# RWKV groups: the next group's key projection right behind the states, other scratch buffers at a group's end, and both squares on ScalarE

## The reference, cut to what matters

```python
def rwkv7_mixer(p, h, v_first, vres, n_ctx, mu, ...):
    shifted = concat([nbr_mean_seq(p[:, :n_ctx]), nbr_mean_grid(p[:, n_ctx:])])
    p = p + mu * (shifted - p)                       # "mixing" with neighbours
    r, k, v, wd_f, wd_b, ad_f, ad_b, gd = split_sizes(p, RWKV_SIZES)
    if vres is not None:
        v = v + (v_first - v) * sigmoid(v0 + (h @ v_down) @ v_up)
    g = sigmoid(gd) @ g_up
    kk = heads(k * k_k, H)
    kk = kk * rsqrt(sum(kk * kk, -1) + L2_EPS)       # square number one
    ...                                              # decays and a, per direction
    o = bidir_prefix(rwkv7_scan, dirs[0], dirs[1], s0, n_ctx)
    var = mean(square(o - mean(o)), -1)              # square number two
    o = merge_heads((o - mean) * rsqrt(var + eps)) * lnx_w + lnx_b
    bonus = (sums over r * k_d * r_k) * v_h
    y = (o + bonus) * g
```

## Time and profile before

| | |
|---|---|
| three runs | 2348.57, 2356.98, 2362.03 us |
| the profiled execution's own time | 2357.53 us |
| its span | 2355.7 us |
| mean granted TensorE clock | 0.962 of full |
| PE (TensorE matmul) busy | 2165.9 us (92%) |
| PEld (weight load) | 1829.6 us (78%) |
| DVE (VectorE) | 1349.7 us (57%) |
| ACT (ScalarE) | 970.6 us (41%) |
| POOL (GpSimd) | 371.9 us (16%) |

### The profile page before, as it was taken

One profiled execution on the slowest core, in us unless ns is written; L12 is line 12 of the kernel. 1 busy time (PEld: TensorE's weight loads), 2 busy tenths in 40 slices (PEclk: granted clock), 3 DMA queues, 4 the chain that ended last, 5 costly groups with the idle time before them and its releaser, 6 DMA issues. The chain is left out here.

```text
span 2355.7 us, 50157 instructions
## 1 busy us (share of the span) xinstructions
PE 2165.9 (92%) x21268; PEld 1829.6 (78%) x21268; DVE 1349.7 (57%) x1956; ACT 970.6 (41%) x1385; POOL 371.9 (16%) x347
## 2 busy tenths in 40 slices
PE   7887999999999999999999998878898988998998
PEld 3565778778787688878888877667887877898998
DVE  5436575665566443464444466477666555567666
ACT  4534233232554232342322347444443454445444
POOL 0002322422333200000000000131232255100000
PEclk9898999999999999999999998999999999999999
DMA  7531413423211223322222233200000122355553
GB/s 282 201 125 59 154 65 110 142 69 135 81 58 55 77 94 98 139 81 98 99 95 94 98 137 106 84 21 29 20 12 29 33 77 68 116 184 189 178 179 126
DMA packets 64734, 241.32 MB, mean 102 GB/s; under 512 B 7296, under 2 KB 8448, under 8 KB 63104
## 3 DMA queue, kind: packets, MB, share of 16 engines
q1 hardware_dynamic: 62064, 218.66, 27.3%
q10 hardware_dynamic: 2448, 19.46, 2.2%
HBM read 231.80 MB, written 6.29 MB: 101 GB/s over the span
## 5 line engine op out<-in xcount | busy, mean ns | idle before, releaser
L397 PE MATMUL psum<-normed_high,weights_high 128*128 128x512 f32 (+1 forms) x1552 | 568.7, 366 | 16.7 <-DVE weight_ring_parts L1042 13.7
L1042 DVE TENSOR_TENSOR weight_ring_parts<-weight_ring,weights_high 128x1024 fp32r<-128x1024 f32 (+1 forms) x327 | 413.2, 1264 | 261.3 <-ACT weights_high L1559 254.1
L398 PE MATMUL psum<-normed_low_part,weights_high 128*128 128x512 f32 (+1 forms) x1552 | 554.4, 357 | 0.0
L399 PE MATMUL psum<-normed_high,weight_ring_parts 128*128 128x512 f32 (+1 forms) x1552 | 553.1, 356 | 0.0
L1559 ACT ACTIVATE weights_high<-weight_ring 128x1024 fp32r<-128x1024 f32 (+1 forms) x327 | 339.9, 1040 | 187.6 <-PE psum L399 136.7
L397 PEld LDWEIGHTS psum<-normed_high,weights_high 128*128 128x128 f32 x1552 | 305.3, 197 | 74.2 <-DVE weight_ring_parts L1042 25.4
L398 PEld LDWEIGHTS psum<-normed_low_part,weights_high 128*128 128x128 f32 x1552 | 305.4, 197 | 40.4 <-issue 2.3
L399 PEld LDWEIGHTS psum<-normed_high,weight_ring_parts 128*128 128x128 f32 x1552 | 303.9, 196 | 40.5
L470 PEld LDWEIGHTS psum<-work 64*64 64x64 f32 x7040 | 233.9, 135 | 35.3 <-issue 24.5
L470 PE MATMUL psum<-work 64*64 64x64 f32 (+1 forms) x7040 | 243.0, 224 | 19.6 <-issue 7.6
L397 PE MATMUL psum<-hidden_high,weights_high 128*128 128x512 f32 (+1 forms) x512 | 172.4, 337 | 3.7 <-DVE hidden_low L1501 3.7
(11 more groups left out here) (241 smaller groups left out, 3217.4 us busy)
## 6 DMA issues: line engine op xcount, KB each, us to landing
weight_ring<-in_weights SPq DMA_DIRECT2D x407, 512.0 KB, 3.5
x_scratch<-work ACTq DMA_DIRECT2D x2, 2048.0 KB, 10.0
weight_ring<-in_weights SPq DMA_DIRECT2D x16, 256.0 KB, 2.6
work<-x_scratch ACTq DMA_DIRECT2D x2, 2048.0 KB, 9.3
work<-in_ret_constants ACTq DMA_DIRECT2D x2, 1152.0 KB, 14.9
work<-in_x ACTq DMA_DIRECT2D x1, 2048.0 KB, 10.0
work<-in_small_weights ACTq DMA_DIRECT2D x1, 1152.0 KB, 5.1
constants<-in_constants ACTq DMA_DIRECT2D x1, 1024.0 KB, 7.2
```

The costliest lines, as they stand in the source:

```text
L397: mm(ps, w[0][:, cols], x[0], start=first, stop=False)
L398: mm(ps, w[0][:, cols], x[1], start=False, stop=False)
L399: return mm(ps, w[1][:, cols], x[0], start=False, stop=last)
L1042: tt(ring_r[:, i % RING, o], ring[:, i % RING, o], high[:, n % HIGHS, o].bitcast(F32), ALU.subtract).then_inc(vec_split.sem, vec_split.ste ...
```

## The change

The key projection of group c+1 moves ahead of the low-rank matmuls on TensorE, and its copies, its mix and its `kk` move ahead of the low-rank work on ScalarE and VectorE. The products of line 1263 stay where they were. The group's end of groups 0 to 2 works in buffers of the two directions that are free by then (`T_OUT`, `T_SQ`, `T_RMS`, `T_BONUS`), and so do two scratch tiles of the values in layer 1, so the pads of `RW_SCR` stay zero and are written once per layer. ScalarE makes both squares in place of GpSimd, and waits for `kk` in its order ahead of a table load and the decays. Group 0 of a layer also has `keys(0)` ahead of `low_rank_parts(0)` on VectorE.

```diff
 # TensorE
 for c in range(NT):
-    project(big, big_filled, split("rw", l, c, 1), ("rkv", l, c, 1))
     if c == 0:
+        project(big, big_filled, split("rw", l, c, 1), ("rkv", l, c, 1))
         eng.wait_ge(act_rwkv.sem, act_rwkv.at("small ready", l))
         for d in range(2):
             low_rank(c, d)
     project(big, big_filled, split("rw", l, c, 0), ("rkv", l, c, 0), lo)
-    eng.wait_ge(pool_rwkv.sem, pool_rwkv.at("kk squared", l, c))
+    eng.wait_ge(act_rwkv.sem, act_rwkv.at("kk squared", l, c))
     big.start_at(2)
     sum_over(bones, wk(RW_SQ), ("kk norm", l, c))
     project(second, big_filled, split("rw", l, c, 2), ("rkv", l, c, 2))
...
-    big.start_at(0)
+    big.start_at(0 if c == NT - 1 else 3)
     if c < NT - 1:
+        project(big, big_filled, split("rw", l, c + 1, 1), ("rkv", l, c + 1, 1))
         low_rank(c + 1, 0)
...
-    eng.wait_ge(pool_rwkv.sem, pool_rwkv.at("centred squared", l, c))
-    sum_over(bones, wk(RW_SCR + 512)[:, lo:N], ("var", l, c), w)
+    eng.wait_ge(act_rwkv.sem, act_rwkv.at("centred squared", l, c))
+    sum_over(bones, wk(T_SQ[c])[:, lo:N], ("var", l, c), w)

 # VectorE
+def keys(c):
+    k = wk(RW_RKV + 512)
+    mix(4 + c, k, ("mixed", l, 4 + c))
+    ts(wk(RW_KK), k, pcol(l, "kk", c), None, ALU.mult)...
+keys(0)
 low_rank_parts(0)
 decayed(0)
 for c in range(NT):
-    mix(4 + c, k, ("mixed", l, 4 + c))
-    ts(wk(RW_KK), k, pcol(l, "kk", c), None, ALU.mult)...
...
     vec_rwkv.also(("centred", l, c))
     if c < NT - 1:
+        keys(c + 1)
         low_rank_parts(c + 1)

 # ScalarE
+def keys_squared(c):
+    eng.wait_ge(vec_rwkv.sem, vec_rwkv.at("kk raw", l, c))
+    act(wk(RW_SQ), wk(RW_KK), ACT.Square)...
-if c > 0:
-    eng.wait_ge(pool_rwkv.sem, pool_rwkv.at("pads rwkv", l, c - 1))
-project(1)
 if c == 0:
+    project(0, 1)
     low_rank(c, 0)
     low_rank(c, 1)
+    keys_squared(0)
     tables(LOG_EXP)
     decays(c)
-project(0)
+project(c, 0)
...
 weights_high(split_at["rw", l, c, 2] + 4)
+eng.wait_ge(vec_rwkv.sem, vec_rwkv.at("centred", l, c))
+act(wk(T_SQ[c])[:, lo:N], wk(T_OUT[c])[:, lo:N], ACT.Square)...
 if c < NT - 1:
     tables(SIGMOID)
+    project(c + 1, 1)
     low_rank(c + 1, 0)
     low_rank(c + 1, 1)
+    keys_squared(c + 1)
     tables(LOG_EXP)

 # GpSimd
 for c in range(NT):
     neighbours(4 + c)
-    eng.wait_ge(vec_rwkv.sem, vec_rwkv.at("kk raw", l, c))
-    tt(wk(RW_SQ), wk(RW_KK), wk(RW_KK), ALU.mult)...
     neighbours(c)
...
-    eng.wait_ge(vec_rwkv.sem, vec_rwkv.at("centred", l, c))
-    tt(wk(RW_SCR + 512)[:, lo:N], wk(RW_SCR)[:, lo:N], wk(RW_SCR)[:, lo:N], ALU.mult)...
-    if c < NT - 1:
-        eng.wait_ge(vec_rwkv.sem, vec_rwkv.at("drained", "gate", l, c))
-        pads(c)
```

More of the change, by code:

```diff
@@ L92 @@
     0, 1024, 1536, 2048, 2560, 3072, 3584, 4096, 4608, 5120, 6144, 6656, 7168)
+T_OUT, T_SQ, T_RMS, T_BONUS = (
+    [a] * 3 + [RW_SCR + 512 * i] for i, a in enumerate((RW_D[0] + RR, RW_D[0] + TT, RW_D[1] + RR, RW_D[1] + TT)))
+T_VGATE, T_VDIFF = RW_D[1] + TT, RW_D[1] + RR
 HG_F, HG_Q, HG_K, HG_A, HG_V, HG_T = 6144, 10240, 14336, 18432, 24576, 26624
@@ L1293, in values_gated @@
                         eng.wait_ge(act_rwkv.sem, act_rwkv.at("vgate sigmoid", l, c))
-                        tt(wk(RW_SCR + 512), wk(RW_SCR + 512), wk(RW_SCR), ALU.mult).then_inc(vec_rwkv.sem, vec_rwkv.step())
+                        tt(wk(T_VDIFF), wk(T_VDIFF), wk(T_VGATE), ALU.mult).then_inc(vec_rwkv.sem, vec_rwkv.step())
                         eng.wait_ge(vec_rwkv.sem, vec_rwkv.n)
-                        tt(vv, vv, wk(RW_SCR + 512), ALU.add).then_inc(vec_rwkv.sem, vec_rwkv.step(("v ready", l, c)))
+                        tt(vv, vv, wk(T_VDIFF), ALU.add).then_inc(vec_rwkv.sem, vec_rwkv.step(("v ready", l, c)))
                         eng.wait_ge(vec_rwkv.sem, vec_rwkv.n)
@@ L1376, in _ @@
                     eng.wait_ge(out_filled.sem, out_filled.at("O", l, c, 0))
-                    cp(wk(RW_SCR)[:, lo:N], outb.get("O", l, c, 0)[:, lo:N]).then_inc(vec_rwkv.sem, vec_rwkv.step(("drained", "O", l, c, 0)))
+                    cp(wk(T_OUT[c])[:, lo:N], outb.get("O", l, c, 0)[:, lo:N]).then_inc(vec_rwkv.sem, vec_rwkv.step(("drained", "O", l, c, 0)))
                     eng.wait_ge(vec_rwkv.sem, vec_rwkv.n)
                     eng.wait_ge(out_filled.sem, out_filled.at("O", l, c, 1))
-                    tt(wk(RW_SCR)[:, lo:N], wk(RW_SCR)[:, lo:N], outb.get("O", l, c, 1)[:, lo:N], ALU.add).then_inc(vec_rwkv.sem, vec_rwkv.step(("drained", "O", l, c, 1)))
+                    tt(wk(T_OUT[c])[:, lo:N], wk(T_OUT[c])[:, lo:N], outb.get("O", l, c, 1)[:, lo:N], ALU.add).then_inc(vec_rwkv.sem, vec_rwkv.step(("drained", "O", l, c, 1)))
                     eng.wait_ge(vec_rwkv.sem, vec_rwkv.n)
@@ L1383, in _ @@
                     if c < NT - 1:
+                        keys(c + 1)
                         low_rank_parts(c + 1)
                     eng.wait_ge(big_filled.sem, big_filled.at("bonus", l, c))
-                    tt(wk(RW_SCR + 1536)[:, lo:N], big.get("bonus", l, c)[:, 0:w], vv[:, lo:N], ALU.mult).then_inc(vec_rwkv.sem, vec_rwkv.step(("drained", "bonus", l, c)))
+                    tt(wk(T_BONUS[c])[:, lo:N], big.get("bonus", l, c)[:, 0:w], vv[:, lo:N], ALU.mult).then_inc(vec_rwkv.sem, vec_rwkv.step(("drained", "bonus", l, c)))
                     eng.wait_ge(vec_rwkv.sem, vec_rwkv.n)
                     eng.wait_ge(act_rwkv.sem, act_rwkv.at("rwkv rms", l, c))
-                    tt(wk(RW_SCR)[:, lo:N], wk(RW_SCR)[:, lo:N], wk(RW_SCR + 1024)[:, lo:N], ALU.mult).then_inc(vec_rwkv.sem, vec_rwkv.step())
+                    tt(wk(T_OUT[c])[:, lo:N], wk(T_OUT[c])[:, lo:N], wk(T_RMS[c])[:, lo:N], ALU.mult).then_inc(vec_rwkv.sem, vec_rwkv.step())
                     eng.wait_ge(vec_rwkv.sem, vec_rwkv.n)
-                    ts(wk(RW_SCR)[:, lo:N], wk(RW_SCR)[:, lo:N], pcol(l, "lnw", c), pcol(l, "lnb", c), ALU.mult, ALU.add).then_inc(vec_rwkv.sem, vec_rwkv.step())
+                    ts(wk(T_OUT[c])[:, lo:N], wk(T_OUT[c])[:, lo:N], pcol(l, "lnw", c), pcol(l, "lnb", c), ALU.mult, ALU.add).then_inc(vec_rwkv.sem, vec_rwkv.step())
                     eng.wait_ge(vec_rwkv.sem, vec_rwkv.n)
-                    tt(wk(RW_SCR)[:, lo:N], wk(RW_SCR)[:, lo:N], wk(RW_SCR + 1536)[:, lo:N], ALU.add).then_inc(vec_rwkv.sem, vec_rwkv.step())
+                    tt(wk(T_OUT[c])[:, lo:N], wk(T_OUT[c])[:, lo:N], wk(T_BONUS[c])[:, lo:N], ALU.add).then_inc(vec_rwkv.sem, vec_rwkv.step())
                     eng.wait_ge(vec_rwkv.sem, vec_rwkv.n)
                     eng.wait_ge(big_filled.sem, big_filled.at("gate", l, c))
-                    tt(wk(Y[0] + 512 * c)[:, lo:N], wk(RW_SCR)[:, lo:N], big.get("gate", l, c)[:, 0:w], ALU.mult).then_inc(vec_rwkv.sem, vec_rwkv.step(("drained", "gate", l, c)))
+                    tt(wk(Y[0] + 512 * c)[:, lo:N], wk(T_OUT[c])[:, lo:N], big.get("gate", l, c)[:, 0:w], ALU.mult).then_inc(vec_rwkv.sem, vec_rwkv.step(("drained", "gate", l, c)))
                     eng.wait_ge(vec_rwkv.sem, vec_rwkv.n)
@@ L1750, in low_rank, with project @@
                         act_rwkv.also(("a sigmoid", l, c, d))
-                    def project(j):
+                    def project(c, j):
                         eng.wait_ge(big_filled.sem, big_filled.at("rkv", l, c, j))
@@ L1782, in _ @@
                         eng.wait_ge(act_rwkv.sem, act_rwkv.n)
-                    project(2)
+                    project(c, 2)
                     for d in range(2):
@@ L1789, in _ @@
                                 eng.wait_ge(big_filled.sem, big_filled.at("vgate", l, c))
-                                act(wk(RW_SCR), first.get("vgate", l, c), ACT.Sigmoid, bias=pcol(l, "v0", c)).then_inc(act_rwkv.sem, act_rwkv.step(("drained", "vgate", l, c)))
+                                act(wk(T_VGATE), first.get("vgate", l, c), ACT.Sigmoid, bias=pcol(l, "v0", c)).then_inc(act_rwkv.sem, act_rwkv.step(("drained", "vgate", l, c)))
                                 tables(LOG_EXP)
@@ L1821, in _ @@
                     weights_high(split_at["rw", l, c, 2] + 4)
+                    eng.wait_ge(vec_rwkv.sem, vec_rwkv.at("centred", l, c))
+                    act(wk(T_SQ[c])[:, lo:N], wk(T_OUT[c])[:, lo:N], ACT.Square).then_inc(act_rwkv.sem, act_rwkv.step(("centred squared", l, c)))
+                    eng.wait_ge(act_rwkv.sem, act_rwkv.n)
                     if c < NT - 1:
                         tables(SIGMOID)
+                        project(c + 1, 1)
                         low_rank(c + 1, 0)
                         low_rank(c + 1, 1)
+                        keys_squared(c + 1)
                         tables(LOG_EXP)
                     eng.wait_ge(big_filled.sem, big_filled.at("var", l, c))
-                    rsqrt(act_rwkv, wk(RW_SCR + 1024)[:, lo:N], big.get("var", l, c)[:, 0:w], 1.0 / 64, "ln", ("rwkv rms", l, c),
+                    rsqrt(act_rwkv, wk(T_RMS[c])[:, lo:N], big.get("var", l, c)[:, 0:w], 1.0 / 64, "ln", ("rwkv rms", l, c),
```

12 lines of the change are left out of this document (5 added, 7 removed).

## The result

The changed kernel took 2377.4 us (median of 4 runs, 2373.01 to 2379.06); the kernel before, with a fourth run beside these, 2353.83 us (2348.57 to 2362.03). The ratio is 1.0094, 95% interval 1.0072 to 1.0115: slower by 17 to 27 us. The forecast was slower, 2371, with 2352 to 2384 as its range. The profiled execution took 2379.06 us, its span is 2377.2, 21.5 more than before.

A forecast was written before the change was run, and what follows sets the result against it. VectorE's order was taken to bound the group borders: +25.2 us at six borders, +0.9 for the clock, -11.5 in group 0, -0.6 in group 3, sum +14.0 on the median 2356.98, so 2371; range 2352 to 2384, own bounds 2363 to 2379.

The forecast's parts named there:

- VectorE bounds the border: Border of two groups: VectorE's gapless order up to line 1042, not GpSimd's square, sets when the value projection starts.
- The border's sum: Six borders between groups: each +4.2 us from later scans less work moved forward and collisions, +25.2 us in all.
- The clock's share: Value projection at the borders: starts cold again, half-clock stretch about as long; +0.15 us each, +0.9 us for six.
- Collisions on VectorE: Border: GpSimd's query sums now fall beside VectorE's multiplications, +0.70 us in layer 0; the PSUM rule would free 0.2 to 0.3.
- The table sets: ScalarE's kk square under the sigmoid's set might need a load of about 1.28 us; the sum would then be 2373.
- Group 0: First group of each layer: keys first on VectorE, first Gram 5.9 and 5.6 us earlier, together -11.5 us, no clock loss taken.
- Group 3: Last group of each layer: ScalarE's square replaces TensorE's 0.50 us wait for GpSimd; 0.4 and 0.2 off, -0.6 us.
- ScalarE's cover: Border: kk's square on ScalarE costs nothing because the root is ready before VectorE wants it; without cover, +0.7 us a border.
- The clock pays for it: Rival: norm sum runs early, value projection finds full clock, 2.1 us a border; 2358, no change; chance 0.20.
- VectorE isn't the bound: Rival: line 1042 through by 325.5, value projection 2.8 us earlier at full clock; 2316; chance 0.13, fully or in part.
- The projection stays cold: Rival: half clock through all 24 value projection matmuls, +28.1 us, 2386; chance 0.12 shared with group 0 gaining nothing.
- The square is not where it hurts: Rival: something else holds group 0's Gram, nothing gained there; 2383; chance 0.12 shared with the projection staying cold.

The follow-up runs named there:

- The run with early weights: Changed kernel with VectorE making the low part of the next group's value weights between its two additions to the inverse product, groups 0 to 2: 2349.86 us, ratio 0.9973.
- the three borders where it was filled: Layer 0 borders of the changed kernel with TensorE making the key norm sum eight times in groups 1 to 3: 2373.86 us, ratio 1.0077.
- The filled run: Early weights, keys after low rank at borders, split value projection (2317.21 us), plus group 0's norm sum three times (layer 0) and six (layer 1): 2309.59 us, ratio 0.9812.
- the first four experiments: Follow-up kernels measured beside the kernel before at 2356.23 us; among them keys first in group 0 alone, 0.9978, and the change with group 0 put back, 1.0128.

## Why the prediction was right, and where its size was off

- *VectorE bounds the border.* Right. Its idle time behind the drain was put at about 5.6 us and is 5.43. The scans were to slip by 8.4 us and slipped by 8.2; the value projection was to be 4.2 us later and is 4.0 in layer 0, 3.8 in layer 1. The run with early weights shows that the gate was line 1042 and its place.
- *The border's sum.* With the clock's share 26.1 us were worked out, and 23.8 measured. The clock's share was shared out wrongly: value projection to Gram is 0.6 us longer in layer 0 and 0.5 shorter in layer 1. That its half-clock part costs about 2.4 us is shown in the three borders where it was filled.
- *Collisions on VectorE.* The query sums of GpSimd were priced at +0.70; the two instructions beside them took 0.98 and 1.10 instead of 0.69 each, +0.70. Both have both inputs in the working memory. The rule of "SBUF — State Buffer" (Trainium skill, "Who interferes with whom") would take nothing off here: the instructions with an input in PSUM (lines 1396 and 1406) had ended before GpSimd began at 319.37.
- *The table sets.* No load came with the squares: 64 table loads in either trace, all asked for by the program. kk's square (312.08) stands between the last sigmoid and the next load (312.74), so it ran while the sigmoid's set was loaded. The load that the prediction feared from "ScalarE: Activation LUTs" (Trainium skill, "Table sets") did not occur.
- *Group 0.* Right at the Gram: -11.5 forecast, -12.1 measured. The step that was mis-sized stands behind it: "I take nothing, the lower end: the key, low-rank, query and value work runs there without a long gap before". TensorE idled 2.45 us in layer 0 and 4.58 in layer 1 ahead of the Gram, the granted clock behind it was 0.59 and 0.50 over 4.2 us, and the Gram's stage lost 1.6 and 2.1 us. The prediction's own bound was 1.5 each. The filled run shows that the clock is the cause of 1.1 and 1.6 us of it; the other 0.9 us stays at full clock.
- *Group 3.* -0.6 forecast. From the drain to the variance sum it is 2.19 us in layer 0 (2.65 before) and 1.44 in layer 1 (1.69 before), -0.7 together: right, though the total of no kernel could show it.
- *The total.* +14.0 was forecast, the interval is 17 to 27, the medians are 23.6 apart, and 2371 lies under all four runs. The median is still within the forecast's own range, 2363 to 2379, but not by merit of its bounds: they stand for collisions, clock and ScalarE's cover at the borders, and the borders came out 2.3 us under their sum. The difference lies elsewhere. The stage of group 0's Gram explains 3.7. The groups' inner parts add 5.2 in the profiled execution, with unchanged code, and the stretches outside 0.9. They differ like that from kernel to kernel: group 1 of layer 0, first Gram to drain, took 65.4 us before, 63.7 changed, and 64.4, 66.2, 66.2 and 67.1 in the first four experiments. Low-clock stretches of some 3 to 7 us begin in the levels of the inverse, now in one group and now in another. Whether the change makes them more frequent stays open.
- *The rivals.* "The clock pays for it" is excluded by the clock row above. "VectorE isn't the bound" is excluded by the 6.79 us of waiting for line 1046. "The projection stays cold" was half right: 5.8 us of it near the lower level, not all. "The square is not where it hurts" is excluded by the 12.1 us that the first Grams of group 0 gained.

## What to carry to other kernels

A wait that costs 35 us in a table of waits is worth only what the next wait leaves: look for the engine without a gap and ask what stands late in its order. When work is pulled ahead on such an engine, count the time that it will wait for its input there, since all that was queued behind now waits too; and when an operation moves to another engine, look at what stands behind its wait in that engine's program (here a table load). An instruction that gates another engine, as the split of the weights does, belongs where its own engine is idle: the same line was worth 28 us in one order and 8 in the other.

## What the runs showed of the hardware

- A gap of 2.45 us on TensorE was followed by a granted clock of 0.59 over 4.2 us, and three gaps of 2.31 and 2.32 us (norm sum eight times, layer 1) by 0.60 to 0.61 over 4.3 us; a gap of 0.77 us was followed by 1.00. The length of the gap alone doesn't tell: in the changed kernel with early weights gaps of 3.29 us were followed by 1.00 twice and by 0.50 once, and of 1.93 us by 1.00.
- The norm sum repeated as mere filling shortened the stage behind it: by 2.4 us at a border of layer 0, and by 1.1 and 1.6 us in the two group 0s. Where it ended 2.3 us too early, at the borders of layer 1, it won nothing. The times of these two kernels point the same way, but their intervals overlap those of the kernels without the filling.
- VectorE's pair of products took 2.14 us beside GpSimd's square and 1.42 without it.
